# Two-layer hybrid decoder on one core: LayerNorm in two passes with a joint table, weight halves placed around it, and an accumulator begun from residual plus embedding

## What is computed

```python
mix = token_mixer(h, ...)
h = layer_norm(ALPHA * h + mix, ln1_g, ln1_b)
ffn = peer_ffn(h, ...)      # 8 heads x 16 chosen experts per token, rows gathered from two tables
ple = sigmoid(h @ ple_gate) * (p @ ple_proj)
h = layer_norm(ALPHA * h + ffn + ple, ln2_g, ln2_b)

def layer_norm(x, g, b):
    mu = mean(x); var = mean(square(x - mu))
    return (x - mu) * rsqrt(var + LN_EPS) * g + b
```

## Time and profile before

| | |
|---|---|
| median of 3 runs | 2176.77 us (2174.72 to 2176.99) |
| span of the profiled execution | 2174.5 us |
| PE busy | 1833.6 us (84%) |
| DVE busy | 1416.6 us (65%) |
| ACT busy | 1025.8 us (47%) |
| POOL busy | 760.4 us (35%) |
| DMA | 656.28 MB, mean 302 GB/s |
| loads of an ACT table at L825 / L826 | 20 / 20, 1.28 us each |

### The profile page before, as it was taken

The page is one execution under the profiler, slowest core; times in us unless marked ns, Lnnn a source line. Parts: engine busy times, 40 slices in busy tenths (PEclk is TensorE's granted clock), DMA queues, the critical chain, the costliest instruction groups (busy, mean ns, idle before and its releaser), DMA issues. The chain is left out here.

```text
span 2174.5 us, 29162 instructions
## 1 busy us (share of the span) xinstructions
PE 1833.6 (84%) x7040; PEld 1080.4 (50%) x7040; DVE 1416.6 (65%) x3386; ACT 1025.8 (47%) x2321; POOL 760.4 (35%) x604
## 2 busy tenths in 40 slices
PE   8999998978778788788799999989787887888776
PEld 7987776932222222223288877769322322322222
DVE  5764465587777777776567535555877776877764
ACT  5743444444454444445347344544545544444443
POOL 0010000135555556665300100001466565565562
PEclk9999999999999999999989999999999999999999
DMA  7411444689999999999744124446799999999996
GB/s 258 143 60 60 153 137 146 221 351 427 428 427 428 427 426 428 428 427 428 330 139 146 46 78 136 140 161 242 289 427 428 428 427 427 427 428 427 428 427 292
DMA packets 105487, 656.28 MB, mean 302 GB/s; under 512 B 11712, under 2 KB 11840, under 8 KB 39232
## 3 DMA queue, kind: packets, MB, share of 16 engines
q0 software_dynamic: 74592, 542.36, 59.3%
q1 hardware_dynamic: 30816, 112.91, 15.5%
HBM read 654.17 MB, written 1.05 MB: 301 GB/s over the span
## 5 line engine op out<-in xcount | busy, mean ns | idle before, releaser
L567 PE MATMUL acc<-arena 128*128 128x512 f32 x1536 | 755.8, 622 | 239.3 <-ACT arena L898 238.4
L487 POOL DMA_INDIRECT arena<-experts_dram,stage x384 | 541.3, 1410 | 337.0 <-PE acc L567 228.1
L1215 DVE CUSTOM_DVE_ANT_0 arena<-arena,h 128x1024 f32<-128x1024 f32 x384 | 471.1, 1227 | 253.2 <-DMA arena<-experts_dram,stage 163.0
L567 PEld LDWEIGHTS acc<-arena 128*128 128x128 f32 x1536 | 270.2, 192 | 713.8 <-issue 712.9
L892 ACT ACTIVATE gel<-dots 128x1 f32<-128x1 f32 x512 | 103.1, 201 | 519.6 <-DVE dots L1215 519.0
L1121 DVE TENSOR_TENSOR raw_r<-raw,w_hi 128x1024 fp32r<-128x1024 f32 x200 | 236.6, 1221 | 148.0 <-ACT w_hi L834 146.8
L567 PE MATMUL acc<-hidden,arena 128*128 128x512 f32 x512 | 251.9, 627 | 27.2 <-ACT arena L898 25.8
L834 ACT ACTIVATE w_hi<-raw 128x1024 fp32r<-128x1024 f32 x200 | 202.8, 1053 | 126.6 <-DMA raw<-weights_dram 96.7
L898 ACT ACTIVATE arena<-cst,gw 128x128 f32<-128x128 f32 x512 | 205.6, 402 | 88.1 <-ACT gw L895 41.9
L487 POOL DMA_INDIRECT hidden<-experts_dram,stage x128 | 161.4, 1261 | 136.4 <-PE acc L567 101.4
L1215 DVE CUSTOM_DVE_ANT_0 hidden<-hidden,h 128x1024 f32<-128x1024 f32 x128 | 156.9, 1228 | 66.5 <-issue 39.5
(11 more groups left out here) (248 smaller groups left out, 2241.7 us busy)
## 6 DMA issues: line engine op xcount, KB each, us to landing
raw<-weights_dram SPq DMA_DIRECT2D x208, 512.0 KB, 3.4
arena<-experts_dram,stage POOLq DMA_INDIRECT x384, 13.7
lnr<-lnrows_dram POOLq DMA_DIRECT2D x4, 1024.0 KB, 5.2
hidden<-experts_dram,stage POOLq DMA_INDIRECT x128, 13.7
cst<-consts_dram SPq DMA_DIRECT2D x1, 1640.0 KB, 15.1
par<-params_dram POOLq DMA_DIRECT2D x2, 616.0 KB, 10.5
h<-x_dram SPq DMA_DIRECT2D x2, 512.0 KB, 5.2
out_dram<-h SPq DMA_DIRECT2D x2, 512.0 KB, 5.3
```

The costliest lines, as they stand in the source:

```text
L487: nc.gpsimd.indirect_dma_start(slots[i % RING][:, :], None, experts[:, :], bass.IndirectOffsetOnAxis(stage[:, i:i + 1], 0)).then_inc(slot_ ...
L567: last = mm(acc[:, c * 512:(c + 1) * 512], diag[:, i % 4, :], slots[i % RING][:, D + c * 512:D + (c + 1) * 512], start=False, stop=ends)
L1215: nc.vector.tensor_tensor_reduce(slots[s][:, 0:D], slots[s][:, 0:D], h[:, b, :], 1.0, 0.0, ALU.mult, ALU.add, dots[:, i:i + 1]).then_inc(d ...
```

## The change

The LayerNorm becomes two passes: (x - mean) * g, which needs no rstd, and then * rstd + b. It takes a source and a destination; for block 1 of ln2 the source is the PSUM accumulator, which PE now begins from identity x `base` instead of zero, so that the two adds are gone (block 0 keeps them). PE waits for `base_ready` there, and for `h2_ready` in place of `acc_drained` at block 0. ACT gets an explicit load of the table set that holds both natural logarithm and exponential (`roots`), at softplus, the first `tr`, the first `mT`, both `onorm`, ln2 of block 1, and ahead of block 0's ln2 in head 6. The splits of the first wq group are placed anew: on ACT at out(0,1), out(1,1) twice, pp(0,0); on DVE at out(1,0) and three at pp(0,1). The order of `pp` and `h1T` changes, and pp(1,1) goes behind wq(0,0). The next layer's first group is split on DVE in head 7 of block 1, after rows 3, 6, 9 and 12.

```diff
-    s += [("pp", 0, 0), ("pp", 1, 0), ("h1T", 0, 0), ("h1T", 0, 1), ("pp", 0, 1), ("h1T", 1, 0), ("h1T", 1, 1), ("pp", 1, 1)]
-    s += [("wq", u, p) for u in range(2) for p in range(2)] + [("sc", b, g) for g in range(2) for b in range(2)]
+    s += [("pp", 0, 0), ("h1T", 0, 0), ("h1T", 0, 1), ("pp", 1, 0), ("h1T", 1, 0), ("h1T", 1, 1), ("pp", 0, 1)]
+    s += [("wq", 0, 0), ("pp", 1, 1), ("wq", 0, 1), ("wq", 1, 0), ("wq", 1, 1)] + [("sc", b, g) for g in range(2) for b in range(2)]
...
@@ splits (ACT)
+        if st[0] == ("out", 1, 0):
+            places = (("out", 0, 1), ("out", 1, 1), ("out", 1, 1), ("pp", 0, 0))
+        else:
+            places = (st[0],) * 4
...
@@ lo_splits (DVE)
+        places = (early, early, late, late)
         if st[0] == ("out", 1, 0):
-            early = late = ("out", 1, 1)
+            places = (("out", 1, 0), ("pp", 0, 1), ("pp", 0, 1), ("pp", 0, 1))
...
@@ PE, experts
-                        if L or b:
-                            pe.wait_ge(acc_drained, L * NB + b)
+                        if b:
+                            pe.wait_ge(acc_drained, L + 1)
+                            pe.wait_ge(base_ready, L * NB + 2)
+                        elif L:
+                            pe.wait_ge(h2_ready, L * NB)
                         for c in range(2):
-                            mm(acc[:, c * 512:(c + 1) * 512], zero, cst[:, 0:512], start=True, stop=False)
+                            left, right = (ident, base[:, 1, c * 512:(c + 1) * 512]) if b else (zero, cst[:, 0:512])
+                            mm(acc[:, c * 512:(c + 1) * 512], left, right, start=True, stop=False)
...
@@ ACT
+            def roots():
+
+                nc.scalar.preload_act_table_set("natural_log_exp_and_others")
...
+                    if step in (("softplus",), ("tr", 0, 0), ("mT", 0, 0), ("ln2", 1)) or kind == "onorm":
+                        roots()
...
                                 if i == 2 and beside == "norm":
+                                    roots()
                                     act.wait_ge(var_ready, L * 4 + 3)
...
@@ DVE, norm
+                last = STT(r, src, mv[:, 0:1], lnr[:, 0:D], ALU.subtract, ALU.mult)
+                link(last)
                 yield
                 dve.wait_ge(rstd_ready, n)
-                link(TS(r, r, mv[:, 0:1], rstd[:, 0:1], ALU.subtract, ALU.mult))
-                yield
-                link(TT(r, r, lnr[:, 0:D], ALU.mult))
-                yield
-                TT(h[:, b, :], r, lnr[:, D:2 * D], ALU.add).then_inc(ready, 1)
+                STT(h[:, b, :], r, rstd[:, 0:1], lnr[:, D:2 * D], ALU.mult, ALU.add).then_inc(ready, 1)
...
@@ DVE, ln2
+                        if b:
+                            layer_norm(acc[:, :], base[:, 1, :], 1, L * 4 + 4, h2_ready)
+                            continue
...
@@ DVE, experts (head 7 of block 1 is called with beside = "split")
+                                if beside == "split" and i % 3 == 2 and i // 3 < len(first_group(L + 1)):
+                                    split_lo(*first_group(L + 1)[i // 3])
```

More of the change, by code:

```diff
@@ L178, in splits @@
     order = [i for i, g in enumerate(GROUPS) if g[1]]
-    at = {GROUPS[a][0][0]: b for a, b in zip(order, order[1:])}
-    at["out", 1, 1] = at.pop(("out", 1, 0))
+    at = {}
+    for a, b in zip(order, order[1:]):
+        st = GROUPS[a][0]
+        if st[0] == ("out", 1, 0):
+            places = (("out", 0, 1), ("out", 1, 1), ("out", 1, 1), ("pp", 0, 0))
+        else:
+            places = (st[0],) * 4
+        for j, step in enumerate(places):
+            at.setdefault(step, []).append((b, j))
     return at
@@ L190, in lo_splits @@
         early, late = st[0], st[len(st) // 2]
+        places = (early, early, late, late)
         if st[0] == ("out", 1, 0):
-            early = late = ("out", 1, 1)
-        at.setdefault(early, []).extend([(b, 0), (b, 1)])
-        at.setdefault(late, []).extend([(b, 2), (b, 3)])
+            places = (("out", 1, 0), ("pp", 0, 1), ("pp", 0, 1), ("pp", 0, 1))
+        for j, step in enumerate(places):
+            at.setdefault(step, []).append((b, j))
     return at
@@ L398, in split_at @@
         def split_at(L, step):
[L400 to L403, removed]
+            return [(L, piece) for piece in SPLIT_AT.get(step, ())]
         def first_group(L):
@@ L1096, in select_head, with norm @@
                 TS(wts[:, bass.ds(g * TOPK, TOPK)], texp, trec[:, 0:1], None, ALU.mult).then_inc(idx_ready, 1)
-            def norm(r, b, n, ready):
-                nc.vector.bn_stats(bst[:, 0:6], r[:, 0:512])
-                link(nc.vector.bn_stats(bst[:, 6:12], r[:, 512:1024]))
+            def norm(src, r, b, n, ready):
+                nc.vector.bn_stats(bst[:, 0:6], src[:, 0:512])
+                link(nc.vector.bn_stats(bst[:, 6:12], src[:, 512:1024]))
                 yield
@@ L1105, in norm, with layer_norm @@
                 yield
+                last = STT(r, src, mv[:, 0:1], lnr[:, 0:D], ALU.subtract, ALU.mult)
+                link(last)
                 yield
                 dve.wait_ge(rstd_ready, n)
-                link(TS(r, r, mv[:, 0:1], rstd[:, 0:1], ALU.subtract, ALU.mult))
-                yield
-                link(TT(r, r, lnr[:, 0:D], ALU.mult))
-                yield
-                TT(h[:, b, :], r, lnr[:, D:2 * D], ALU.add).then_inc(ready, 1)
-            def layer_norm(r, b, n, ready):
-                for _ in norm(r, b, n, ready):
+                STT(h[:, b, :], r, rstd[:, 0:1], lnr[:, D:2 * D], ALU.mult, ALU.add).then_inc(ready, 1)
+            def layer_norm(src, r, b, n, ready):
+                for _ in norm(src, r, b, n, ready):
                     pass
@@ L1130, in _ @@
                         for piece in first_group(0):
-                            split_lo(*piece)
-                    if step == ("ln2", 1):
-                        for piece in first_group(L + 1):
                             split_lo(*piece)
@@ L1178, in _ @@
                         dve.wait_ge(acc_filled, L * NB + b + 1)
-                        dve.wait_ge(base_ready, L * NB + b + 1)
+                        if b:
+                            layer_norm(acc[:, :], base[:, 1, :], 1, L * 4 + 4, h2_ready)
+                            continue
+                        dve.wait_ge(base_ready, L * NB + 1)
                         for c in range(2):
                             cs = slice(c * 512, (c + 1) * 512)
-                            last = TT(base[:, b, cs], base[:, b, cs], acc[:, cs], ALU.add)
+                            last = TT(base[:, 0, cs], base[:, 0, cs], acc[:, cs], ALU.add)
                         last.then_inc(acc_drained, 1)
-                        dve.wait_ge(acc_drained, L * NB + b + 1)
-                        if b:
-                            layer_norm(base[:, b, :], b, L * 4 + 2 + b + 1, h2_ready)
+                        dve.wait_ge(acc_drained, L + 1)
                         continue
@@ L1208, in head @@
                             elif beside == "norm":
-                                choose = norm(base[:, 0, :], 0, L * 4 + 3, h2_ready)
+                                choose = norm(base[:, 0, :], base[:, 0, :], 0, L * 4 + 3, h2_ready)
                             for i in range(TOPK):
@@ L1225, in _ @@
                             head(EH - 2, "norm", False)
-                            head(EH - 1, None, False)
+                            head(EH - 1, "split", False)
                         continue
```

2 lines of the change are left out of this document (1 added, 1 removed).

## The result

| | before | after |
|---|---|---|
| time, median (lowest to highest) | 2175.83 us (2174.72 to 2176.99) | 2146.75 us (2146.16 to 2148.99) |
| ratio with its 95% interval | | 0.9866 (0.9852 to 0.9880) |
| span of the profiled execution | 2174.5 us | 2144.3 us |
| table loads on ACT | 155 | 127 |

The forecast was 2153.6 us, in a range of 2148.5 to 2161.0. The change is faster, as forecast, but by 30.2 us in the spans where the sum had 23.2. On another chip the changed kernel gave 2146.91 (2141.02 to 2150.44) beside 2172.84 of the kernel before, ratio 0.9884 (0.9867 to 0.9901), 25.9 us between the medians. So the saving is 26 to 29 us, and the sum was 3 to 6 us short.

What follows compares the result with a forecast made beforehand. Gathers on full DMA queues bound the expert stage, PE the dense part. Savings 3.9 + 4.9 + 2 x 7.2 = 23.2 from 2174.5 give 2151.3; with 2.3 for the runs' median, 2153.6 us, range 2148.5 to 2161.0.

Steps and rivals of the forecast that it cites:

- ln1: First LayerNorm of each layer, worked on layer 1: 7.2 us saved per layer, bounds 5.5 to 8.3.
- The end: Kernel end, last matmul to h: 4.2 us against 8.16, so 3.9 us saved, 3.7 to 4.0 with PSUM reads.
- the h term: ln2 of block 1 in layer 0: h 4.95 us earlier, 3.9 as at the end plus 1.06 from moved splits.
- rival D: Clock returns early between the layers and never falls at wq: 27.5 us saved, 2149.3 us; chance 0.11.
- steps (a) to (c): In ln1: one split before out(1,0), 0.3 late; block 0's h at 1430.2; block 1's h at 1435.3, 9.5 us earlier.
- (d): PE's work in ln1 meanwhile, pp(0,1) ending at 1438.4, its bank drained late behind the fourth weight half, done at 1436.1.
- the 8.0 of the mechanism: In ln1, wq(0,1) starts at 1448.0 instead of 1450.0 + 6.0: 8.0 us earlier, before the clock loss of 0.8.
- The remaining preloads: Softplus, tr, onorm, experts: loads of 1.28 saved on ACT with no PE wait on them; 0, at most 1 us in all.
- B: PE waits longer before wq(0,0), from a late fourth-half load or falling clock: 3 us per layer, 2159.6 us; chance 0.10.
- C: Joint table not taken up, a load remains between Ln and Exp: 5.5 us less gain, 2159.1 us; chance 0.08.
- E: Expert stage start waits for something that does not shift, both ln1 gains vanish: 8.8 left, 2168.0 us; chance 0.05.
- F: Piece behind pp(1,1) lands late, PE stands before wq(1,1): at 22 us delay price 31.4, 2185.0 us; chance 0.06.

Runs made afterwards that it cites:

- the first trace: The changed kernel as first profiled, against the kernel before: span 2144.3 us, median 2146.75 us, ratio 0.9866.
- the second: The changed kernel itself run once more, unaltered: median 2146.91 us, span of the profiled execution 2139.2 us.
- the placement alone: The kernel before with only the new order of pp, h1T and wq and new places of the first wq group's halves: 2169.80 us, ratio 0.9973.

## Why the prediction was right in sign and short in size

In short: two terms were too small. ln1 was worth 8.8 to 8.9 us per layer and not 7.2, since the fourth weight half was held to the latest landing of its load that the trace of before has, and 0.8 was taken off for a clock that did not fall. The preloads ahead of tr, put at nothing, gained 2.5 us. Against that, 0.9 was lost behind ln2.

**The end, 3.9: right** (3.9). From PSUM the statistics take 0.70 and 0.68 and the pass 1.27, from SBUF (layer 1's ln1) 0.69, 0.68 and 1.28; the lower bound of 3.7 was not needed. The accumulator's two starting matmuls cost nothing that shows.

**ln2 of block 1: the h term right** (4.95 forecast, 4.96 measured), with the cover for the splits in the last head as forecast; the run that undid it lost 1.04 where I had 1.06. What stayed open, the clock behind it, went against the change in the first trace: the stretch at 1.2 GHz lasted 9.2 us behind PE's restart instead of 7.3, and 0.9 us was given back; in the second it lasted 6.8 and 0.2 was gained. The net of 4.0 and 5.2 is inside 3.4 to 7.6. (The lower bound had 1.5 us for a slow stretch that falls wholly on matmuls; at half the clock it costs half of what was wait before, (7 - 5.34) / 2 = 0.8.) That full clock might return early (part of rival D) did not happen.

**ln1: mechanism right, term mis-sized.** Forecast 7.2, measured 8.84 and 8.91 in the first trace, 8.69 and 9.72 in the second. The steps (a) to (c) hold to 0.1 us: out(1,1) is evicted 0.2 after PE begins the embedding products, h is there 5.15 after it (forecast 5.1), and no load stands between Ln and Exp. Two steps failed:
- In (d) I had the fourth high half end at 1436.1, the time it had before, 5.9 after that start. In the first trace it ended 5.2 after the start, in the second 4.3. The evictions behind it came earlier with it, and PE's wait before wq(0,0) was 1.09 and 0.28 instead of the 1.8 to 2.0 forecast. That is 0.7 to 1.7 per layer. The load is issued at a fixed distance from PE, as I had it; what I took for fixed was the time it needs to land. Layer 1 of before, on which I worked, is the latest of the sixteen (4.83 after the start), and "layer 0 has the same distances" was wrong for this row: there the half started at 3.13. With the half at 4.83 the rule above gives a wait of 1.8, as forecast, so the chain behind the load was right. Why one landing takes longer than another no run shows.
- The 0.8 taken off for the clock was the middle of two observations with waits of 1.8 to 2.0. With a wait of 1.1 or less the clock stayed at 1.00 in both layers. Without that 0.8 the term is 8.0, and with the wait 0.8 shorter it is 8.8, which is what was measured.

In all six kernels with PE's long wait for h (4.7 to 8.6) a stretch at 1.2 GHz follows in both layers, and in none of the seven traces with waits of 0.2 to 1.4 does one. So the 8.0 of the mechanism rightly held the return of the clock: transposes 1.06 instead of 1.94, embedding product 1.88 instead of 3.54.

**The remaining preloads, "0, at most 1": wrong.** In tr of layer 0 they gained 1.5 in the first trace (0 in the second, where the clock fell there), and in layer 1 1.0 and 0.8. I looked for a PE wait that names ACT; there is none that shortens by such a size. By the ledger the 1.5 comes in four steps of 0.15 to 0.7 us at two places (L654 and L667 of before); that these stand at the end of a chain (Ln, Exp, DVE's scaling, ACT's evictions) is how I read it. The run without them shows the eight loads and DVE's waits of 1.9 come back; that the gain is the preloads' is shown by all thirteen traces together, as above.

**The stages between.** The clock stretch of the earlier trace rows ahead of W_out in layer 1 is absent from both traces of the changed kernel, 1.2 us in the first. It is also absent from the placement alone and from the run without tr's preloads, and present in the other variants of the changed kernel, with the same work ahead of it; so I take it for scatter and no effect of the change. The rest, 0.25 at the start and 0.4 and 0.15 in the expert stages, is of the size by which two executions differ.

The sum again, with the terms of the first trace: 3.9 + 4.1 (4.96 less the 0.9 given back) + 8.84 + 8.91 + 2.5 for the preloads (1.5 and 1.0) = 28.2, and 1.8 for the stages between and 0.13 for PE's first matmul make 30.2, the difference of the spans.

**The rivals.** B (a late fourth half, 3 us per layer): the opposite. C (no joint table): no load is left between Ln and Exp. The Trainium skill (ScalarE: Activation LUTs, "Table sets"), by which one set holds ln and exp, agrees with the rows: one load at 2134.91 serves both. D (2149.3) is the nearest, yet not for its reason: the clock stayed up at wq, but not behind ln2, and the rest came from tr and from the shorter wait before wq(0,0). E and F: between wq(0,0) and the first gather the list of PE's waits is empty in both layers, and in layer 1 that gather moved from 1504.92 to 1478.82. PE's wait for weights, which F priced, does not appear. The range was too narrow below since its upper bound for ln1 was the bare mechanism, with no room for a wait that turns out shorter, and since edits costed at "at most 1" were held to it without a row.

## What to carry over

An event that a transfer releases has two parts, the issue, which moves with the engine that frees the slot, and the landing, which here took 4.0 to 6.0 us for the same load: look it up at every place where the trace has it (here layer 0 and layer 1 differed by 1.7 us) before one value goes into the sum. Parts that shorten one chain do not add up; two passes and the joint table overlap (5.1 us are saved where they give 2 x 2.0 and 2 x 1.28 alone), while moving work away from a norm pays nearly twice as much once the norm is short (4.2 to 5.0 against 2.3 to 2.9 per layer). And where ACT and DVE wait for each other in turn, count ACT's table loads as path time even if no single wait of PE names them.

## What the runs showed of the hardware

- A one-tensor pass of DVE over 1024 columns takes 0.81 us from SBUF and 1.34 from PSUM, while the two-tensor pass (scalar_tensor_tensor) takes 1.28 from SBUF and 1.27 from PSUM. The Trainium skill (VectorE: DVE Perf Modes, "Why PSUM operands drop a tier") says that on PSUM input the faster modes fall away; it agrees with the first pair. The second pair takes from SBUF about what the first takes from PSUM, and loses nothing. So reading the accumulator is free for the two-pass norm and would have cost 0.53 with the old one.
- Waits of PE of 0.2 to 1.4 us at ln1 left the granted clock at 2.4 GHz; behind those of 4.7 us and more it fell to 1.2 GHz. Behind waits of 1.8 to 2.1 elsewhere (at 86, 173 and 323 us) both happened, in two executions of one and the same program, whose spans differ by 5.1 us.
- A weight load of 512 KB, issued 1.17 us ahead of the same matmul each time, let ACT start 4.0 to 6.0 us after its issue.
